# Down weights in 4 MB transfers, ring slots renumbered, first gate earlier, last expert scattered alone

## What is computed

```python
hb = x_pad[tok_blk] @ w1[e] + b1[e]          # up: 1024 -> 2048
ob = clamped_swiglu(hb) @ w2[e] + b2[e]      # down: 1024 -> 1024
return ob * w_blk[:, None].astype(ob.dtype)
...
h = h + moe_ffn(rms_norm(h, norm_ffn[i]), ...)
return rms_norm(h, norm_final)[:, N_META:]
```

## Time and profile before

| | us |
|---|---|
| median of 3 runs | 1308.57 (1308.5 to 1308.95) |
| the profiled execution | 1309.25 |
| its span | 1307.4 |

### The profile page before, as it was taken

How to read it: one execution, slowest core, us unless ns; L and a number is a source line. 1 busy time by engine, 2 the same in 40 slices (tenths; PEclk the granted TensorE clock), 3 DMA queues, 4 the chain that set the end, 5 groups by cost and what they waited for, 6 DMA issues and landing times.

```text
span 1307.4 us, 17754 instructions
## 1 busy us (share of the span) xinstructions
PE 1279.9 (98%) x7143; PEld 643.4 (49%) x7143; DVE 470.8 (36%) x1127; ACT 337.6 (26%) x653; POOL 27.4 (2%) x40
## 2 busy tenths in 40 slices
PE   9999999999999999999999999999999999999997
PEld 7888888899983333333333323333333333333332
DVE  5979899987653111211112111112111112111112
ACT  4767777654441101111011011011011011001102
POOL 1000000022010000000000000000000000000000
PEclk9999999999999999999999999999999999999999
DMA  8333264456879999999999999999999999999996
GB/s 313 121 138 122 80 233 158 190 206 239 344 306 421 423 402 428 428 429 429 429 431 433 431 432 426 431 433 430 433 430 427 432 433 431 431 431 431 426 426 282
DMA packets 32181, 467.24 MB, mean 357 GB/s; under 512 B 4113, under 2 KB 4145, under 8 KB 8705
## 3 DMA queue, kind: packets, MB, share of 16 engines
q1 hardware_dynamic: 31840, 466.00, 85.5%
q10 hardware_dynamic: 288, 0.52, 0.1%
HBM read 465.43 MB, written 1.08 MB: 357 GB/s over the span
## 4 chain that ended last, share of the span: by engine, by line
PE 46%; DMA 23%; DVE 0%; SPq 0%; ACT 0%; issue 0%; DVEq 0%
PE bank L1564 44%; DMA ring<-wts_dram 16%; DMA work<-wts_dram 7%; PE bank L1948 1%; PE bank L1942 1%; PE bank L1972 1%; SPq L430 0%; SPq L564 0%; DVE work L1558 0%; DVE work L1524 0%; ACT work L976 0%; DVE work L1540 0%; DVE work L1468 0%; DVEq L107 0%; DVE work L1470 0%
## 5 line engine op out<-in xcount | busy, mean ns | idle before, releaser
L1564 PE MATMUL bank<-ring,work 128*64 128x512 f32 (+2 forms) x2152 | 488.7, 587 | 11.9 <-DMA ring<-wts_dram 11.8
L1564 PE MATMUL bank<-work 128*64 128x512 f32 (+8 forms) x2216 | 437.1, 548 | 6.3 <-DMA work<-wts_dram 4.3
L1564 PEld LDWEIGHTS bank<-ring,work 128*64 128x64 f32 (+1 forms) x2152 | 155.8, 138 | 295.3 <-issue 261.8
L1564 PEld LDWEIGHTS bank<-work 128*64 128x64 f32 (+4 forms) x2216 | 148.1, 143 | 263.9 <-issue 245.9
L1564 PE MATMUL bank<-hn_hi,split 128*128 128x256 f32 (+1 forms) x896 | 173.0, 288 | 1.6 <-DVE work L1300 1.4
L1491 DVE COPY work<-bank 128x256 f32<-128x256 f32 x30 | 12.7, 424 | 449.3 <-PE bank L1972 449.3
L1564 PEld LDWEIGHTS bank<-hn_hi,split 128*128 128x128 f32 x896 | 141.5, 189 | 2.7 <-DVE work L1300 1.6
L1564 PE MATMUL bank<-hn_lo,split 128*128 128x256 f32 (+1 forms) x448 | 127.2, 284 | 0.0
L1072 DVE TENSOR_TENSOR split<-ring,split 128x1024 fp32r<-128x1024 f32 x88 | 109.7, 1249 | 24.2 <-ACT split L662 23.8
L1468 DVE TENSOR_SCALAR work<-bank 128x512 f32<-128x512 f32 x32 | 22.1, 692 | 262.3 <-PE bank L1564 262.3
L903 ACT ACTIVATE work<-bank 128x512 f32<-128x512 f32 x31 | 18.5, 597 | 325.6 <-PE bank L1564 325.6
(11 more groups left out here) (301 smaller groups left out, 948.8 us busy)
## 6 DMA issues: line engine op xcount, KB each, us to landing
ring<-wts_dram SPq DMA_DIRECT2D x83, 2048.0 KB, 18.2
ring<-wts_dram SPq DMA_DIRECT2D x20, 4096.0 KB, 30.3
work<-wts_dram SPq DMA_DIRECT2D x20, 4096.0 KB, 29.3
ring<-slabs_dram SPq DMA_DIRECT2D x23, 2048.0 KB, 8.5
work<-wts_dram SPq DMA_DIRECT2D x23, 2048.0 KB, 13.5
ring<-wts_dram SPq DMA_DIRECT2D x7, 1024.0 KB, 17.4
ring<-decay_rows SPq DMA_DIRECT2D x16, 256.0 KB, 3.4
work<-wts_dram SPq DMA_DIRECT2D x4, 1024.0 KB, 11.4
```

The source lines that it names most:

```text
L1564: return pe.matmul(o, lhsT, rhs, start=start, stop=stop)
```

## The change

- From expert 9 to 29, both units of the down weights come in one transfer (`load_down_pair`), after `down_done`. `down` then waits once, at k = 0. In DRAM the two units of an expert's down weights are interleaved by partition, as the up weights are.
- The ring slots are numbered anew: up in 2, 3, 0, 1 and down in 4, 5. Which unit goes into a slot changes, the times at which slots become free do not. The half that comes last before the experts is now of down weights.
- The second down unit of expert 30 comes in two halves.
- The first gate (`gate_of(0)`) stands ahead of `lo_of(PZ + 2)` on VectorE.
- Expert 30 is scattered inside the last down, at k = 2; `scatter_last` adds expert 31 with four matmuls of 64 rows.
- At the end VectorE squares bank 0 and GpSimd scales it; both reciprocal roots are computed together.

```diff
-W1_SLOT = [3, 4, 1, 2]
-W2_SLOT = [5, 0]
+W1_SLOT = [2, 3, 0, 1]
+W2_SLOT = [4, 5]
...
+            def load_down_pair(e, t):
+
+                sp.wait_ge(down_done, t)
+                sp.dma_start(w2_pair.rearrange("p (i c) -> p i c", i=2), pair_of(e, 2)).then_inc(w2_in[0], 16)
+
...
             sp.wait_ge(*used["so3"])
-            load_w2(0, 1)
+            load_w1(0, 2, False)
...
             sp.wait_ge(*used["wout0"])
+            load_w1(0, 0, False)
+            sp.wait_ge(*used["wout1"])
             load_w1(0, 3, False)
-            sp.wait_ge(*used["wout1"])
-            load_w1(0, 2, False)
             sp.wait_ge(wout_used, 5)
-            load_half(0, 1, 1, False)
+            load_w2_half(0, 1)
             sp.wait_ge(wout_used, 6)
-            load_w2_half(1)
+            load_w2_half(1, 1)
             sp.wait_ge(wout_done, 4)
-            load_half(0, 1, 0, False)
+            load_w2_half(0, 0)
...
             for e in range(2 * TURN, E - 3):
                 odd = (e + 1) % 2
                 ahead = 1 if e < 20 else 0
                 load_pairs(e + 3, e + 3, odd, range(ahead))
-                load_down(e + 1, e + 1)
+                load_down_pair(e + 1, e + 1)
...
-            load_down(E - 2, E - 2)
+            sp.wait_ge(down_used, E - 2)
+            load_w2(E - 2, 0)
+            sp.wait_ge(down_done, E - 2)
+            for at, arrival in ((0, w2_in[1]), (UNIT // 2, slab_in[0])):
+                sp.dma_start(w2_sb[1][:, at:at + UNIT // 2], unit_of(E - 2, W1_UNITS + 1)[:, at:at + UNIT // 2]).then_inc(arrival, 16)
...
+            pool.wait_ge(nfin_in, 32)
+            pool.wait_ge(h2_copied, 1)
+            pool.tensor_tensor(fin[:, 0, 0:512], h2_copy, nfin[0][:, :], ALU.mult).then_inc(h2_scaled, 1)
...
+            for b, n in ((0, 1), (1, 0), (1, 1)):
                 a.wait_ge(scattered, 2 * b + n + 1)
                 a.activation(hsq_end[:, b, n * 512:(n + 1) * 512], bank[2 * b + n][:, :], ACT.Square,
...
+            a.wait_ge(ssh_ready, 1)
+            a.activation(root2, ssh[:, :], ACT.Sqrt, scale=1.0 / D, bias=eps_col).then_inc(ms_ready, 1)
...
             xdt_of(1)
+            gate_of(0)
             lo_of(PZ + 2)
...
+            d.wait_ge(scattered, 1)
+            d.tensor_copy(h2_copy, bank[0][:, :]).then_inc(h2_copied, 1)
+            d.wait_ge(h2_copied, 1)
+            d.tensor_tensor_reduce(out=hsq_end[:, 0, 0:512], in0=h2_copy, in1=bank[0][:, :], scale=1.0, scalar=0.0,
+                                   op0=ALU.mult, op1=ALU.add, accum_out=ssh4[:, 0, 0:1]).then_inc(h2_dve_squared, 1)
...
-            def scatter_pair(t, r):
+            def scatter_last(t, r):
+                pe.wait_ge(scat_ready, t + 1)
                 for b in range(2):
+                    for n in range(2):
+                        rows = slice(n * SLOTS, (n + 1) * SLOTS)
+                        pe.wait_ge(*((ob_ready, t + 1) if n else (last_ob_ready, r + 1)))
+                        mm(bank[2 * b + n][:, :], scat_last[rows, b * P:(b + 1) * P], ob_last[rows, :], False, True).then_inc(scattered, 1)
...
-                down(t0 + E - 1, 4, actT_last, lambda: None, later=r is not FIRST, final=r is FIRST)
-                scatter_pair(t0 + E - 2, r)
+                down(t0 + E - 1, 4, actT_last, lambda: scatter(t0 + E - 2), later=r is not FIRST, final=r is FIRST, paired=r is not FIRST)
+                scatter_last(t0 + E - 1, r)
```

More of the change, by code:

```diff
@@ L417, in unit_of @@
             def unit_of(e, u):
-                return pair_of(e, u // 2)[:, u % 2, :] if u < W1_UNITS else wts[bass.ds((e * E_UNITS + u) * P, P), :]
+                return pair_of(e, u // 2)[:, u % 2, :]
             def load_w1(e, u, odd):
@@ L919, in actT_of, with ob_of @@
                                  scale=0.5).then_inc(actT_ready, 1)
-                def ob_of(t, whole):
+                def ob_of(t):
                     a.wait_ge(down_done, t + 1)
[L923 to L927, removed]
+                    a.activation(ob[:, :], bank[6][:, :], ACT.Copy).then_inc(ob_ready, 1)
                 def step(t, gathers, routing):
@@ L1277, in ysum_of, with gate_of @@
                 d.tensor_tensor(ysq[:, c % 4 - 1, :], ysq[:, c % 4 - 1, :], ysq[:, c % 4, :], ALU.add).then_inc(ysum_ready, 1)
+            def gate_of(c):
+                d.wait_ge(z_tanh, c + 1)
+                d.scalar_tensor_tensor(zw, ztanh[:, c % 2, :], 1.0, bank[U["z", c] % 2][:, 0:SEQ], ALU.add,
+                                       ALU.mult).then_inc(proj_read, 1)
             diff_of(0)
@@ L1298, in _ @@
                     d.wait_ge(y2_ready, c)
-                d.wait_ge(z_tanh, c + 1)
-                d.scalar_tensor_tensor(zw, ztanh[:, c % 2, :], 1.0, bank[U["z", c] % 2][:, 0:SEQ], ALU.add,
-                                       ALU.mult).then_inc(proj_read, 1)
+                    gate_of(c)
                 if c + 1 < NX:
@@ L1536, in _ @@
             d.wait_ge(nfin_in, 32)
[L1538 to L1550, removed]
[L1551 to L1556 removed]
+            d.wait_ge(scattered, 1)
[3 more added lines that the diff above has]
+                                   op0=ALU.mult, op1=ALU.add, accum_out=ssh4[:, 0, 0:1]).then_inc(h2_dve_squared, 1)
+            d.wait_ge(h2_squared, 1)
+            d.tensor_tensor(fin[:, 0, 512:D], bank[1][:, :], nfin[1][:, :], ALU.mult).then_inc(h2_scaled, 1)
+            d.wait_ge(h2_squared, 3)
+            d.wait_ge(h2_dve_squared, 1)
+            d.tensor_tensor(ssh[:, :], ssh4[:, :, 0], ssh4[:, :, 1], ALU.add).then_inc(ssh_ready, 1)
+            d.wait_ge(ssh_ready, 1)
+            link(d.tensor_scalar(ms2, ssh[:, :], 1.0 / D, EPS, ALU.mult, ALU.add))
+            d.wait_ge(ms_ready, 1)
+            y, tmp = rsh[:, :], nrt[:, 0:2]
+            link(d.reciprocal(y, root2))
+            link(d.tensor_tensor(tmp, y, y, ALU.mult))
+            link(d.scalar_tensor_tensor(tmp, ms2, -0.5, tmp, ALU.mult, ALU.mult))
+            d.scalar_tensor_tensor(y, tmp, 1.5, y, ALU.add, ALU.mult).then_inc(rsh_ready, 1)
+            d.wait_ge(rsh_ready, 1)
             for n in range(2):
@@ L1993, in up @@
                     if k % (2 if single else 4) == 0:
-                        in_halves = k == (0 if odd else 2)
+                        in_halves = odd and k == 0
                         extra_use = in_halves + (1 if later and not odd and k == 0 else 0)
@@ L2006, in up, with down @@
                 last.then_inc(up_done, 1)
-            def down(t, to=6, actT=actT, between=None, first=None, later=False, final=False):
+            def down(t, to=6, actT=actT, between=None, first=None, later=False, final=False, in_halves=False, paired=False):
                 halves = [w2_sb[0][:, 0:UNIT // 2], w2_sb[0][:, UNIT // 2:UNIT], w2_sb[1][:, 0:UNIT // 2], w2_sb[1][:, UNIT // 2:UNIT]]
@@ L2026, in down @@
                         pe.wait_ge(extra_in[k - 6], 32)
-                    elif k == 4:
-                        pe.wait_ge(w2_in[1], 16 * t if later else 16 * (t + 1))
+                    elif in_halves and k == 6:
+                        pe.wait_ge(slab_in[0], 16 * (len(NEIGHBOURS[0]) + 1))
+                    elif k == 4 and not paired:
+                        pe.wait_ge(w2_in[1], 16 * (SINGLE + 1) if in_halves else 32 if first == 0 else 16 * (t + 2))
                     elif first == 1 and k in (0, 2):
@@ L2034, in down @@
                         at = k % 2 * 1024 + j * 512
-                        at_rows = 1 - j if to == 4 else j
-                        last = mm(bank[to][at_rows * SLOTS:(at_rows + 1) * SLOTS, :], actT[:, k % 4, (k // 4) * SLOTS:(k // 4 + 1) * SLOTS],
+                        last = mm(bank[to][j * SLOTS:(j + 1) * SLOTS, :], actT[:, k % 4, (k // 4) * SLOTS:(k // 4 + 1) * SLOTS],
                                   halves[k // 2][:, at:at + 512], k == 0, k == KD - 1)
@@ L2070, in step @@
                     if gathers:
-                        down(t, first=first, later=r is not FIRST)
+                        down(t, first=first, later=r is not FIRST, paired=last_up or not single)
                     else:
                         pe.wait_ge(scat_ready, t + 1)
-                        down(t, between=lambda: last_transposes(t + 1), later=r is not FIRST)
+                        down(t, between=lambda: last_transposes(t + 1), later=r is not FIRST, in_halves=r is FIRST, paired=r is not FIRST)
                 def first_between(k):
```

60 lines of the change are left out of this document (17 added, 43 removed).

## The result

| | before | after |
|---|---|---|
| median of 11 runs each | 1309.13 us (1308.5 to 1310.72) | 1311.5 us (1310.17 to 1314.97) |
| the profiled execution | 1309.25 | 1311.14 |
| its span | 1307.4 | 1309.4 |

The ratio is 1.0018, 95% interval 1.0011 to 1.0026: +2.4 us (+1.4 to +3.4). The forecast was 1310.0 with a range of 1305.5 to 1313.2. The difference is real and small. The ratio is inside the 0.2% that the prediction called the same, though the median of 1311.5 is 0.3 above the 1311.2 at which it drew that line: the kernel before came out 0.56 slower here than in the three runs that the forecast starts from.

A forecast was written before the change was run, and what follows sets the result against it. The prediction took the experts to be bound by the stream of weights. Its terms, 0 - 1.0 + 2.2 - 0.3 + 0.5 = +1.4, on the median of 1308.57 gave 1310.0 us, range 1305.5 to 1313.2.

The forecast's parts named there:

- Step 1: New ring slots and loads ahead of the experts: same amounts issued at the same waits, 0 us.
- Step 2: Stream pace over experts 9 to 29: 4 MB down transfers slightly faster than two of 2 MB, -1.0 us.
- Rival C: 4 MB down transfers cost no less than two units, so no pace gain: 1311.0 us; chance 0.05.
- Step 3: Down weights issued later and waited for whole: queue thins at experts 13 and 21, 1.1 us each, +2.2 us.
- Step 4: First gate ahead of the split on VectorE: TensorE's wait of 1.35 us shrinks, -0.3 us.
- Step 5: The end: scatter inside last down, shorter last scatter, squares on ScalarE, four output writes together, +0.5 us.
- A: Weight queue does not thin enough to matter: 1307.8 us, far end 1304.8; chance 0.25, far end 0.10 more.
- B: TensorE's clock falls at the merged waits before downs 12 and 20: +3.8 us, 1312.4; chance 0.15.

The follow-up runs named there:

- e_end: Kernel before with only the new end (expert 30 scattered inside the last down, `scatter_last`, new normalisation), old loads; 1311.29 us, ratio 1.0018.
- f_norm: Kernel before with only the final normalisation changed (bank 0 squared on VectorE, scaled on GpSimd, both roots at once); 1310.67 us, ratio 1.0010.
- f_tail29: Kernel before with new loads and slots, old gate and end, but expert 29's down weights in two units; 1310.61 us, ratio 1.0006.
- g_three: Kernel before with new loads and slots, old gate and end, but down weights of experts 13, 21, 29 in two units; 1309.64 us, ratio 1.0004.

## Why the prediction was nearly right, and what in it was not

The total was +1.4 against a measured +2.4 (+1.4 to +3.4), so the sum held at its edge. That is in part luck, since two misses cancelled. The loads (steps 2 and 3) were to cost 1.2 and by the landings gained 0.4; the end was to cost 0.5 and cost 1.4; and the changed kernel's stream was 1.1 late by 691 us, which no step had. -0.4 + 1.1 + 1.4 = +2.1, where the spans differ by 2.0.

**Step 1, slots: right.** The first up starts at 400.64 without a wait for DMA, and the loads alone cost at most 2.0 us.

**Step 2, pace -1.0: right, slightly small.** From the down landing at 691.7 to that at 1002.6 are 310.9 us, before 311.9 (690.6 to 1002.5): -1.0. From 1023.1 to expert 29's at 1256.4 are 233.3, before 233.8: -0.5. Together -1.5, within its bounds of 0 and -1.6. Rival C is out. It buys nothing in the time: TensorE in the changed kernel was 0.4 us late at the first expert and the stream 0.7 more by 691, with losses of 0.2 to 0.9 at seven landings between 439 and 555 us, queued 4 to 11 us deep. `e_end` and `f_norm` with their old loads also end up with last landings of 1295.8 and 1295.5 (before: 1295.2), and the landing near 691 us lies between 689.7 and 691.7 in the twelve traces. Such shifts come from run to run.

**Step 3, +2.2: the mechanism was right, the size double.** The place, the 2.5 us of queue and the single wait of 1.7 us came as forecast. The loss was 1.1 at one spot and 0 at the other (in `f_tail29` 0.1 and, at expert 13, 1.5). I read a smooth line from queue depth to loss; the runs show a loss that comes or doesn't, more often in a thin queue. Nor does a loss come back, as I had assumed: the transfer behind the late one lands the usual 9.7 later (1032.8 after 1023.1). And "the margin is above 10 us" from e = 20 on was wrong: the down pairs of experts 22, 23 and 24 had 5.4, 7.1 and 8.9 us queued. In the changed kernel none of them lost anything. Of my sentence that TensorE's whole-pair wait "costs nothing as long as something is queued", the last pair is the exception: behind expert 29 TensorE has 42 us of work without a wait, and what it waits there is paid in full.

**Step 4, gate -0.3: too hopeful.** The timeline answers to the earlier trace rows:

```profile
182.87 0.41 DVE L1280 SCALAR_TENSOR_TENSOR work<-work,bank 128x256 f32<-128x256 f32 x1
183.19 1.22 DVE L1071 TENSOR_TENSOR split<-ring,split 128x1024 fp32r<-128x1024 f32 x1
184.56 0.36 PE L1562 MATMUL bank<-hn_hi,split 128*128 128x256 f32 x1 [0.50 <-DVE split L1071]
189.75 0.38 PE L1562 MATMUL bank<-hn_hi,split 128*128 128x256 f32 x1 [0.63 <-DVE work L1280]
```

One wait of 1.35 became 0.50 and 0.63, as forecast in kind. But the 0.2 between them is not a gain. In the kernel with the gate alone the matmul of the second wait is

```profile
189.40 0.39 PE L1568 MATMUL bank<-hn_hi,split 128*128 128x256 f32 x1 [0.63 <-DVE work L1281]
```

and in the kernel before it starts at 189.35: nothing is left. The first up starts at 400.31 (400.24 before), and the gate alone spans 1307.4, as before.

**Step 5, the end +0.5: too small by 0.9, and it is the cost that the time shows.** It is 1.4 by the trace. Term by term, from the second half of down of expert 30:

- Start of the last scatter: 1299.36 - 1285.91 = 13.45 against 1297.33 - 1285.30 = 12.03: +1.4, forecast +0.9. The scatter inside the last down takes 1.9 us (1291.22 to 1293.13), and the cover was the one wait of 0.41; the second wait of the same size, which I counted without a row, isn't in the trace.
- From there to the last output's issue: 1304.87 - 1299.36 = 5.5 against 1303.91 - 1297.33 = 6.6: -1.1, forecast -0.7 (+0.2 for the squares after a start 0.9 late).
- From that issue to the end: 4.5 against 3.5: +1.0, forecast +0.3. I priced four writes together at half a write's pace; they took the full 1.0 by which two of them went ahead before.

A reading of mine was wrong besides, in the description of the end too: the old `scatter_pair` has four matmuls of 128 rows, one per bank, not eight. Its eight rows of timeline are their halves. The new four have 64 rows each; their eight rows take 1.99 us instead of 3.67. So 1.7 us are saved, as forecast, but not by issuing half as many.

**The model of the end** failed with it: I took the end as the last landing plus a tail. That holds before; after, the chain leaves the stream at 1256.45, and with the new end alone at the half that starts at 1285.89.

**Rivals.** A (no loss at the queue) is half true, one spot of two. B (slower clock in downs 12 and 20) did not happen: both merged waits of 1.7 were followed by full speed. Its kin did happen at expert 29 in two other kernels, and costs 1.7 us there. All traces together say how near it was: ahead of a whole down pair, waits of 0.2 to 1.7 us were followed by 32 matmuls in 7.09, waits of 1.9 us and more by 8.4 to 10.1.

**What stays open:** the 0.6 us ahead of down of expert 30 are within what runs differ by, so their cause is not settled. Why about 1 us is lost at single landings is open too. No version here beats the kernel before clear of noise; the gate alone (0.9996) and `g_three` (1.0004) are level with it.

## What to carry to other kernels

Before you price a stretch by the last landing, ask for each edit whether the chain still runs through it. Here 1.9 us of work went into a wait of 0.41, the waits ended, and the rest counted in full. A whole-buffer wait near the end can hand the end to the engine in the same way. Work put "into a wait" needs a row for each wait that is to hide it. At the very end, writes that leave in two batches finish earlier than the same writes issued together, even if the later batch goes out at the same moment. And before a trace explains a median, ask where its execution lies among the others.

## What the runs showed of the hardware

- The slower clock behind waits of one length comes or stays away, ahead of a first up pair: waits of 1.61 and 1.60 us in the same kernel 29 us apart were followed by 16 matmuls in 3.65 and in 5.35 us. The Trainium skill ("TensorE: Matmul & The Clock Gate", section "HAM oscillation — how this bites in real kernels") has a kernel in which waits for DMA bring it back every time; the traces here agree that a wait can, not that each does. When it comes it takes up the room of 1.7 us, and the wait of the next step is gone.
- 4 MB transfers follow each other every 9.7 us in a queue, and one into an empty queue takes 12.1 to 12.4. The Trainium skill ("DMA: Bandwidth & Descriptors", section "Anatomy of one DMA — SWDGE (gpsimd) path") gives about 2.0 us of fixed cost per transfer, for transfers that GpSimd issues; the 2.4 to 2.7 over the pace seen here, on SyncE's queue and only when it was empty, are near it.
- Now and then a landing is about 1 us late: three of six with 2.5 us queued (1.1, 1.1, 1.5), and also 1.0 to 1.2 at 10.8, 11.2, 15.7 and 18.3 us. The depths don't order the losses; they order how often one comes.
- Four float32 matmuls on 64 rows took 1.99 us where four on 128 rows took 3.67: those on the two halves of the array overlap, as their records begin two at a time, within 0.04 us.
